# Gathering each later expert's rows by an indirect DMA and eight transposes instead of 32 one-hot matmuls

## What is computed

```python
def moe_swiglu(x, w_router, w_gate, w_up, w_down):
    xt = x.reshape(b * s, d)                       # 256 tokens x 1024, RMS-normed
    logits = (xt @ w_router).astype(jnp.float32)
    top_val, top_idx = lax.top_k(logits, TOP_K)    # 2 of 8
    top_w = jax.nn.softmax(top_val, axis=-1)
    gates = jnp.sum(jax.nn.one_hot(top_idx, N_EXPERTS) * top_w[..., None], axis=1)
    y = jnp.zeros_like(xt)
    for e in range(N_EXPERTS):
        y = y + gates[:, e:e + 1] * swiglu(xt, w_gate[e], w_up[e], w_down[e])
```

## Time and profile before

| | |
|---|---|
| runs | 1534.57, 1536.21, 1536.38 us (median 1536.21) |
| profiled execution, span | 1535.3 us (the page gives no other time for it) |
| TensorE matmul busy | 1475.4 us, 96% |
| VectorE busy | 1136.2 us, 74% |
| ScalarE busy | 959.9 us, 63% |
| GpSimd busy | 79.4 us, 5% |
| read from HBM | 423.81 MB |

### The profile page before, as it was taken

How to read it: one execution, slowest core, us unless ns; L and a number is a source line. 1 busy time by engine, 2 the same in 40 slices (tenths; PEclk the granted TensorE clock), 3 DMA queues, 4 the chain that set the end, 5 groups by cost and what they waited for, 6 DMA issues and landing times.

```text
span 1535.3 us, 21503 instructions
## 1 busy us (share of the span) xinstructions
PE 1475.4 (96%) x7978; PEld 1255.1 (82%) x7978; DVE 1136.2 (74%) x825; ACT 959.9 (63%) x863; POOL 79.4 (5%) x80
## 2 busy tenths in 40 slices
PE   6989999999989899999999999999999999999996
PEld 6887999989987688788878878878887887887885
DVE  4474444455374588888888888888888888887886
ACT  5374344345274477767667767767776776776774
POOL 2240000000000000000000000010000000001000
PEclk9999999999999899999999999999999999999999
DMA  9422755555322499999999989989999998998992
GB/s 337 169 83 94 214 191 165 198 183 160 129 83 83 144 367 378 338 329 371 340 324 372 370 305 369 364 332 340 374 342 322 367 359 315 373 375 304 348 366 108
DMA packets 202917, 425.40 MB, mean 277 GB/s; under 512 B 7680, under 2 KB 52992, under 8 KB 202880
## 3 DMA queue, kind: packets, MB, share of 16 engines
q1 hardware_dynamic: 198160, 418.01, 76.2%
q10 hardware_dynamic: 4720, 6.87, 1.6%
HBM read 423.81 MB, written 1.05 MB: 277 GB/s over the span
## 4 chain that ended last, share of the span: by engine, by line
PE 89%; DVE 5%; ACT 3%; issue 2%; DMA 1%; SPq 0%; DVEq 0%; ACTq 0%
PE banks L1106 27%; PE banks L1108 27%; PE banks L1107 27%; PE banks L1366 2%; PE banks L1397 1%; ACT w_hi L409 1%; DVE w_lo L714 1%; PE banks L1264 1%; DMA raw<-in_w_in_e 1%; DVE xn L727 1%; DVE xres L1038 0%; ACT arena L523 0%; DVE qk_lo L1027 0%; PE banks L1162 0%; DVE arena L855 0%
## 5 line engine op out<-in xcount | busy, mean ns | idle before, releaser
L714 DVE TENSOR_TENSOR w_lo<-raw,w_hi 128x2048 fp32r<-128x2048 f32 x397 | 904.1, 2290 | 255.6 <-ACT w_hi L409 255.4
L409 ACT CAST w_hi<-raw 128x2048 fp32r<-128x2048 f32 x397 | 758.6, 1912 | 282.4 <-PE banks L1108 278.4
L1106 PE MATMUL banks<-w_hi,t_hi 128*128 128x512 f32 (+2 forms) x1088 | 418.1, 384 | 5.2 <-DVE w_lo L714 2.7
L1108 PE MATMUL banks<-w_lo,t_hi 128*128 128x512 f32 (+2 forms) x1088 | 411.3, 378 | 0.0
L1107 PE MATMUL banks<-w_hi,t_lo 128*128 128x512 f32 (+2 forms) x1088 | 410.7, 377 | 0.0
L1106 PEld LDWEIGHTS banks<-w_hi,t_hi 128*128 128x128 f32 x1088 | 205.5, 189 | 43.2 <-DVE w_lo L714 4.1
L1108 PEld LDWEIGHTS banks<-w_lo,t_hi 128*128 128x128 f32 x1088 | 205.2, 189 | 38.9
L1107 PEld LDWEIGHTS banks<-w_hi,t_lo 128*128 128x128 f32 x1088 | 205.6, 189 | 36.9 <-issue 0.2
L1106 PE MATMUL banks<-w_hi,h_hi 128*128 128x512 f32 x536 | 209.3, 390 | 0.7 <-DVE w_lo L714 0.7
L1108 PE MATMUL banks<-w_lo,h_hi 128*128 128x512 f32 x536 | 209.2, 390 | 0.0
L1107 PE MATMUL banks<-w_hi,h_lo 128*128 128x512 f32 x536 | 208.7, 389 | 0.0
(11 more groups left out here) (191 smaller groups left out, 1020.6 us busy)
## 6 DMA issues: line engine op xcount, KB each, us to landing
raw<-in_moe_w_gate SPq DMA_DIRECT2D x112, 1024.0 KB, 6.3
raw<-in_moe_w_up SPq DMA_DIRECT2D x112, 1024.0 KB, 6.4
raw<-in_moe_w_down SPq DMA_DIRECT2D x112, 1024.0 KB, 6.6
raw<-in_na_w_qkv SPq DMA_DIRECT2D x12, 1024.0 KB, 5.1
raw<-in_ffn_w_gate SPq DMA_DIRECT2D x11, 1024.0 KB, 5.4
raw<-in_ffn_w_up SPq DMA_DIRECT2D x11, 1024.0 KB, 5.3
raw<-in_ffn_w_down SPq DMA_DIRECT2D x11, 1024.0 KB, 4.9
raw<-in_w_in_e SPq DMA_DIRECT2D x7, 1024.0 KB, 14.9
```

The source lines that it names most:

```text
L409: act.copy(w_hi[:, u.part, 0:n], raw[:, u.raw, 0:n]).then_inc(hi_done, 1)
L714: dve.tensor_tensor(w_lo[:, u.part, 0:n], raw[:, u.raw, 0:n], w_hi[:, u.part, 0:n].bitcast(F32), ALU.subtract).then_inc(lo_done, 1)
L1106: pe.matmul(out, a_hi, b_hi, start=start, stop=False)
L1108: return pe.matmul(out, a_hi, b_lo, start=False, stop=stop)
```

## The change

A copy of `xn` is written to DRAM (`xn_rows`) by two DMAs from GpSimd's queue after the last normalisation ahead of the experts. For each expert but the first: GpSimd makes the one-hot matrix `pick_x` in float32; TensorE multiplies it with a column of token numbers (`slots`, two matmuls of one column) at the start of the preceding expert's last gate_up; VectorE copies the 128 sums to `row_i` as integers (`row_index`), between two `lo`; GpSimd then issues an indirect DMA that fetches 128 rows of 4 KB to `x_tok`; and TensorE turns them by eight transposes (`turn_rows`), at the place where `gather` stood. The first expert keeps `gather`. The table that is loaded at the start is two columns wider. The core of the diff:

```diff
+            def row_index(g):
+                dve.wait_ge(idx_mm, g + 1)
+                dve.tensor_copy(row_i[:], banks[:, 7, SEQ:SEQ + 1]).then_inc(idx_ready, 1)
...
-                for c in (36, 37, 38):
+                lo(unit_of(base, e, 36))
+                if nxt is not None:
+                    row_index(e + sweep * (E - 1))
+                for c in (37, 38):
                     lo(unit_of(base, e, c))
...
+            def slots(v, g):
+
+                pe.wait_ge(pickx_ready, g + 1)
+                pe.wait_ge(y_add, v * 4 + 1)
+                for t in range(T):
+                    last = pe.matmul(banks[:, 7, SEQ:SEQ + 1], pick_x[:, t, :], tab[:, C_TOK + t:C_TOK + t + 1],
+                                     start=(t == 0), stop=(t == T - 1))
+                last.then_inc(idx_mm, 1)
+
+            def turn_rows(g):
+
+                pe.wait_ge(x_tok_in, g * 16 + 16)
+                for k in range(KD):
+                    last = pe.transpose(banks[:, 2 + k // 4, (k % 4) * P:(k % 4 + 1) * P],
+                                        x_tok[:, k * P:(k + 1) * P], ident)
                     if k % 4 == 3:
                         last.then_inc(gath_mm, 1)
...
+                if nxt is not None:
+                    slots(v, e + sweep * (E - 1))
                 gate_up(base, [(e, 34 + i, 0) for i in range(4)])
+                if nxt is not None:
+                    pe.wait_ge(idx_ready, e + sweep * (E - 1) + 1)
                 turn_pick(v)
                 if nxt is not None:
-                    gather(v + 1)
+                    turn_rows(e + sweep * (E - 1))
...
+            for t in range(T):
+                pool.wait_ge(xn_ready, 11 + t)
+                pool.dma_start(rows_d[t * P:(t + 1) * P, :], xn[:, t, :]).then_inc(rows_out, 16)
...
-                if not first:
+                if e == 0 and sweep:
                     for t in range(T):
                         last = pool.tensor_scalar(pick[:, t, :], places, place_e[:, t:t + 1], None, ALU.is_equal)
                     last.then_inc(pick_ready, 1)
+                if e:
+                    for t in range(T):
+                        last = pool.tensor_scalar(pick_x[:, t, :], places, place_e[:, t:t + 1], None, ALU.is_equal)
+                    last.then_inc(pickx_ready, 1)
+                    pool.wait_ge(rows_out, 16 * T)
+                    pool.wait_ge(idx_ready, g + 1)
+                    pool.indirect_dma_start(out=x_tok[:], out_offset=None, in_=rows_d,
+                                            in_offset=bass.IndirectOffsetOnAxis(ap=row_i[:], axis=0)).then_inc(x_tok_in, 16)
```

More of the change, by code:

```diff
@@ L74 @@
 C_ID, C_TRI, C_IOTA, C_ONES = 1152, 1280, 1408, 1664
-C_ALL = 1792
+C_TOK = 1792
+C_ALL = 1794
 def constants():
@@ L101, in constants @@
     c[:, C_ONES:C_ONES + P] = 1.0
+    c[:, C_TOK:C_TOK + T] = pos.reshape(T, P).T
     return c
@@ L238, in trunk @@
         top_i = sb("top_i", [P, T, 8], U32)
+        rows_d = nc.dram_tensor("xn_rows", (SEQ, D), F32, kind="Internal").ap()
+        x_tok = part_of(5120, 1024)
+        pick_x = part_of(6144, 256).rearrange("p (t s) -> p t s", t=T)
+        row_i = sb("row_i", [P, 1], U32)
         over = sb("over", [P, 1], I32)
@@ L286, in trunk @@
         route_step = sem("route_step")
+        rows_out, pickx_ready = sem("rows_out"), sem("pickx_ready")
+        idx_mm, idx_ready, x_tok_in = sem("idx_mm"), sem("idx_ready"), sem("x_tok_in")
         out_sent = sem("out_sent")
@@ L1357, in _, with gather @@
             keep_busy(7, 8)
-            def gather(v):
-                pe.wait_ge(pick_ready, v + 1)
+            def gather(v, sweep):
+                pe.wait_ge(pick_ready, sweep + 1)
                 for k in range(KD):
@@ L1367, in gather @@
                                              start=(t == 0 and i == 0), stop=(t == 1 and i == 1))
+                    if k % 4 == 3:
+                        last.then_inc(gath_mm, 1)
+            def slots(v, g):
[10 more added lines that the diff above has]
+                                        x_tok[:, k * P:(k + 1) * P], ident)
                     if k % 4 == 3:
@@ L1432, in edge @@
                     pe.wait_ge(xn_lo_done, T)
-                    gather(sweep * E)
+                    gather(sweep * E, sweep)
                     clear(0)
@@ L1514, in _ @@
             pool.wait_ge(q_zero, 2)
+            for t in range(T):
+                pool.wait_ge(xn_ready, 11 + t)
+                pool.dma_start(rows_d[t * P:(t + 1) * P, :], xn[:, t, :]).then_inc(rows_out, 16)
             def picks(e, sweep):
                 v = e + sweep * E
+                g = sweep * (E - 1) + e - 1
                 first = v == 0
```

## The result

| | before | changed |
|---|---|---|
| runs (fast), median | 1535.39 us (1532.67 to 1536.38, 4 runs) | 1552.05 us (1550.22 to 1559.18, 4 runs) |
| ratio to before | 1 | 1.0117 (95% interval 1.0096 to 1.0139); of the medians 1.0109 |
| profiled execution: time, span | span 1535.3 us | 1559.18 us, span 1557.3 us |
| mean granted TensorE clock, profiled | 0.992 | 0.980 |

The forecast was 1557 us with a range of 1518 to 1585. The profiled execution is the slowest of the four; the others took 1550.2 to 1553.6 at clocks of 0.985 to 0.987. Over the profiled spans the change costs 22.0 us, over the medians 16.7.

The account below looks back on a forecast made before the run. TensorE was taken to bound the experts. Each edge: -2.36 saved, +3.7 stall, +1.65 clock, +3.0 in all; seven give +21 on 1535.3, 1556.3, and 0.9 more for the median: 1557 us, range 1518 to 1585.

Parts of the forecast that it names:

- the stall: TensorE waits in front of turn_rows for the gathered rows, 3.7 us at each of seven edges between experts.
- What bounds the kernel: In the experts transfers wait for arithmetic, so a microsecond taken from TensorE's queue comes off the span.
- the forecast's own net: TensorE at each edge: 2.91 us saved by transposes replacing one-hot matmuls, less 0.55 for slots; net 2.36 us.
- When the index is ready: VectorE finishes row_index at about 743.1, leaving GpSimd and the DMA 6.5 us before turn_rows can start at 749.67.
- GpSimd's part: Writing descriptors takes 1.0 us of work, only in holes between VectorE's lo operations: done at 748.9.
- a sign of a wrong mechanism: GpSimd's indirect DMA being issued at once in the middle of a lo would show the mechanism wrong.
- The transfer: The 512 KB of rows land 4.5 us after GpSimd's issue, beside the weights' traffic: at 753.4.
- the two bounds of the forecast: Landing of 512 KB at the start: 3.7 us after issue with quiet queues, 9.1 behind another transfer.
- The clock: TensorE's clock falls to half for 3.3 us after each stall, losing 1.65 us an edge.
- Rival 1: Rows arrive in time, GpSimd writing descriptors beside VectorE or fitting ahead of lo 37: 1519.7 us; chance 0.35 with half case.
- Rivals 2 and 3: GpSimd's DMA takes the fourth hole between VectorE's operations (1577 us, chance 0.14), or waits until VectorE runs dry (1597, 0.12).

Follow-up runs that it names:

- early: Changed kernel with each expert's index computed and its indirect DMA issued one expert ahead, turn_rows left in place: 1519.29 us, ratio 0.9894 to before.
- dve_quiet: Changed kernel with VectorE waiting for x_tok right after it wrote row_i, so it is silent while the DMA is issued: 1582.71 us, one execution.
- plain: Changed kernel with a plain GpSimd DMA of rows 0 to 127 in place of the indirect one: 1525.31 us, one execution.
- psum_ops: Changed kernel with three VectorE copies from PSUM to unused SBUF behind row_index, before the next lo: 1538.16 us, ratio 1.0012 to before.
- both_quiet: Changed kernel with the experts' weights loaded by a quarter only and VectorE waiting for x_tok behind row_index: 1554.64 us, one execution.
- dma_quiet: Changed kernel with the experts' weights loaded by a quarter only, all else the same: 1522.48 us, one execution.

## Why the prediction was right, and where its terms were not

The time, the way it moved and the kind of loss (rows that come late, then half clock) were right. Why the rows come late was not, and the number came out by luck: the stall's parts were off by some 2 us each, in opposite senses.

- **What bounds the kernel** and what a removed matmul is worth: right. 2.82 - 0.46 = 2.36 us an edge, the forecast's own net (2.91 - 0.55), where two misses of 0.09 cancel; early shows it as 16.9 us of time.
- **When the index is ready, and that the copy `row_index` costs nothing:** right. It fell in the hole ahead of the second `lo`, 6.8 us ahead of the need (forecast 6.5).
- **GpSimd's part: the step failed, though the blocking it rests on is real.** The forecast had 1.0 us of work that runs only in the holes between VectorE's operations, done 5.7 us after the index. The work is 1.02 us (dve_quiet), but it starts 0.77 us after the index, is held once, until the `w_lo` in progress ends, and then runs on through the next one: done 3.5 to 3.6 us after the index. The prediction named as a sign of a wrong mechanism a DMA issued in the middle of a `lo`; the later part of the record lies in one. The blocking was carried from a copy to the writing of descriptors; plain shows that a plain DMA isn't blocked at all. The box that the prediction cites from the Trainium skill ("SBUF — State Buffer", "SBUF: two separate sides") speaks of VectorE's operations in a two-port mode; `w_lo` isn't one by its terms, since it reads two SBUF inputs, and no run here tests the box. Of an operation with two SBUF inputs that section of the Trainium skill says that it blocks only a GpSimd operation that reads SBUF. The traces agree: the copy took 2179 ns instead of 181 and the indirect DMA, whose index `row_i` lies in SBUF, 2.76 us instead of 1.02, while the plain DMA, which has no index, took 0.6 us either way.
- **The transfer: mis-sized.** Forecast 4.5 us; 6.35 under the weights' traffic and 3.3 with a quarter of it. The measured time lies midway between the two bounds of the forecast, 3.7 and 9.1; the choice nearer the quiet one was the error. The Trainium skill's page "DMA: Bandwidth & Descriptors" ("Anatomy of one DMA") gives an estimate of 3.2 us for this size. The trace agrees with it in the quiet case (3.3) alone.
- These two errors, some 2.1 us too much and 1.85 too little, cancel: landing 9.9 us after the index in the mean, forecast 10.2 (743.2 to 753.4). So the stall, 3.1 us in the mean, came near its forecast of 3.7 by a sum whose parts were wrong. That is luck.
- **The clock:** 1.71 us behind each edge (twice that behind the first), forecast 1.65. The falls behind the scatters, 8.6 us in the profiled execution, were missed: the earlier trace rows had shown no fall after one idle 1.77 us, but the same trace has one, behind the scatter of 1409.2, one of seven.
- **Rivals.** Rival 1 (in time) missed by the stall, 3.1 us an edge, though its condition, that GpSimd works beside VectorE, holds for a plain DMA; even without any blocking the traffic makes the rows late, by 1.7 us an edge in psum_ops. The time of rival 1 is what early makes true, at 1519.3 against its 1519.7. Rivals 2 and 3 rested on the holes and fall with them.

## What to carry to other kernels

A DMA that replaces arithmetic is worth its arithmetic only if its address is known early enough: count from the moment the index exists, add the issue, the transfer at the share that the other traffic leaves, and the landing, and compare with the moment of use. Here 9.9 us stood against 6.8, and the same work issued one expert ahead turned 1.1% slower into 1.1% faster. A stall of TensorE where it bounds the kernel can cost more than its length: behind the seven of 2.4 to 3.7 us the half clock took 13.7 us more.

## What the runs showed of the hardware that I had not expected

- An indirect DMA from GpSimd's queue (128 rows of 4 KB) has a record of 1.02 us, a plain one 0.59. A `w_lo` (a VectorE operation with two SBUF operands) that is in progress when the indirect one begins holds it until it ends (2.76); one that begins 0.14 us later does not (1.02). A plain one isn't held at all.
- Traffic alone doubles a transfer: 512 KB landed 3.3 us after the end of the record with the weights at a quarter, 6.4 with the DMA engines full.
- After a TensorE wait of 2.3 to 4.0 us at an edge the granted clock fell to 1.2 GHz, for 3.4 us or twice that, in 17 of 18 cases (after, psum_ops, both_quiet; the exception is a wait of 3.76 at the first edge of both_quiet); after 11 waits of 0.4 to 1.6 us there (psum_ops, plain, dma_quiet) it did in none. After the 1.77 us ahead of a scatter it fell in 22 of 77 cases over all eleven traces.
